# Routed experts of a decoder trunk: one stream over the experts, and the scatter in two rounded products

## The chip, the cores and the metric

The kernel runs on 1 core of one Trainium2 chip. The metric is the device time of one execution in microseconds (us). The kernel before takes 2135.12 us, the median of 3 runs (2126.69 to 2139.0).

## The reference, cut to what matters

A trunk of two layers over 256 tokens of 1024 channels, all in float32. Both layers have the same token mixing (three attention-like mixers between an input and an output projection). The first ends in a dense SwiGLU, the second in a routed one with 8 experts, of which each token uses 2; the change is in that last part.

```python
def swiglu(h, w1, w3, w2):
    return (jax.nn.silu(h @ w1) * (h @ w3)) @ w2

def moe_ffn(h, w_router, w1, w3, w2):
    logits = (h @ w_router).astype(jnp.float32)
    top_v, top_i = lax.top_k(logits, TOP_K)          # TOP_K = 2
    top_w = jax.nn.softmax(top_v, axis=-1)
    gate = jnp.sum(jax.nn.one_hot(top_i, N_EXPERTS) * top_w[..., None], axis=-2)
    y = jnp.zeros_like(h)
    for e in range(N_EXPERTS):                        # 8; w1[e], w3[e]: 1024 x 3584, w2[e]: 3584 x 1024
        y = y + gate[..., e:e + 1] * swiglu(h, w1[e], w3[e], w2[e])
    return y
```

## The kernel before, in words

**Weights.** Every weight passes through one pipe. The SP queue loads it in chunks of 1 MB (128 partitions of 4 rows of 512 columns) into a ring of 6 buffers `raw` (`load`, L539). Each chunk is two halves. For each half ScalarE writes the rounded fp32 copy `w_hi` (L1234, called by `split_to`), and VectorE writes the remainder `w_lo` = `raw` - `w_hi` (L1568). Both have a ring of 4 halves (`HL`), and `split_to` may stand 3 halves (`AHEAD`) ahead of the half that TensorE is to use next. `w_hi` of a half waits until TensorE has used the half that is 4 before it (`half_used`); a `raw` buffer comes free when `w_lo` of both halves is done (`raw_done`). A product is `mm3` (L677 to L679): three rounded-fp32 matmuls per 128 rows of weight, low part of the left side by `w_hi`, high part by `w_lo`, high part by `w_hi`. `use(n)` on ScalarE and VectorE issues the splits up to 3 halves behind the next n chunks and counts them as passed. So splits stand in the same queue as all the other work of these two engines, in the order in which the program is written.

**The experts.** The tokens of one expert (at most 128 in one item) are gathered by a product with a one-hot matrix `sel` (VectorE makes it, L2051): `gather` forms 8 blocks of `x` transposed in the two banks `pT`, VectorE applies the modulation on the way out (`x_f`, L2060, in `gathered`), ScalarE and VectorE split it into `x_hi` and `x_lo` (L2068). Expert width 3584 is cut into 7 blocks of 512. A block has three products of 4 halves, each half 6 matmuls: gate into `pA[0]`, up into `pA[2]`, and down into the two banks `pO`, which stay open over the whole expert. ScalarE takes silu of the gate into `a_sb` (L1520), VectorE multiplies by the up product (`hidden`, L2081), TensorE transposes the result (`turn_a`, L725, 4 transposes in the banks `pT`), ScalarE and VectorE split it into `aT_hi` and `aT_lo` (`hi_a`, and L2089 in `lo_a`). Inside an expert this is staggered: the gate product of block f stands ahead of the transposes of block f - 1, then the up product of f, then the down product of f - 1.

**Between two experts** the order on TensorE is: down product of block 5 of the expert; `gather` for the next expert; `turn_a` of block 6; its down product; then `scatter`, four fp32 matmuls (two instructions each in the trace) of `selT` (the transposed one-hot) and the output `oe` into the banks `pT`, each of which VectorE multiplies by the gate and adds to `yacc` (L2114); then two transposes of the next `sel` into `selT`, and two matmuls by `zeros` that open the banks `pO`; then the gate product of block 0 of the next expert. ScalarE copies the left half of the output out of `pO`, VectorE the right half (L2109). The body of this loop runs `items` times: 8, or 16 if an expert has more than 128 tokens. Here it is 8.

The few lines on TensorE that stand between the experts:

```python
                        with rounds(pe, 1, EFB, {b.raw: 6, b.hl: 12, b.T: 2, G: 1, U: 1, av: 1}):
                            gate_up(pA[0], G, g_free)
                            turn_a()
                            gate_up(pA[2], U, u_free)
                            down()
                        pe.wait_ge(sel_ready, xv.done(v) + 2)
                        gather()
                        turn_a()
                        down(True)
                        evacuated(b.O, O_free, 2)
```

## Time and profile before

| | before |
|---|---|
| median of the runs | 2135.12 us (2126.69 to 2139.0) |
| time of the profiled execution | 2136.17 us |
| its span, from the first to the last instruction | 2134.4 us |
| TensorE matmul busy | 1991.8 us (93%) |
| TensorE weight load busy | 1576.0 us (74%) |
| VectorE busy | 1526.7 us (72%) |
| ScalarE busy | 1237.3 us (58%) |
| mean granted TensorE clock | 0.962 |
| HBM read | 530.83 MB, 249 GB/s over the span |
| the experts | from 1024 us to 2120 us of the span |

The span is read engine by engine: the page's first part gives each engine's busy time, the fourth the chain of work that ended last. An engine with a high share of busy time can still be free at the place where something waits, so the boundaries between experts are read from the timeline. PE stands for TensorE's matmuls, DVE for VectorE, ACT for ScalarE. Starts are us from the start of the span. An execution takes 1.8 us more than its span.

### The profile page before, as it was taken

The numbers are of one execution on the slowest core, as the hardware profiler recorded it, in microseconds if no ns is written. First come the engines' busy times: TensorE is split into PE (matmuls) and PEld (weight loads), VectorE is DVE, ScalarE is ACT, GpSimd is POOL, SyncE is SP. The second block draws the span as 40 slices with busy tenths as digits, with TensorE's granted clock in tenths as the row PEclk, the third lists the DMA queues.
The fourth block names the chain that finished last, engine by engine and source line by source line (L and its number), as shares of the span: only waits on it lengthen the run. The fifth ranks groups of instructions, "written<-read, shape, count | busy, mean of one in ns | idle before, by whom it ended". The sixth has DMA issues, their size and how long they took to land.

```text
span 2134.4 us, 28418 instructions
## 1 busy us (share of the span) xinstructions
PE 1991.8 (93%) x9524; PEld 1576.0 (74%) x9524; DVE 1526.7 (72%) x1827; ACT 1237.3 (58%) x1590; POOL 90.3 (4%) x133
## 2 busy tenths in 40 slices
PE   5999999899979999997899999999999999999996
PEld 2777887777767777886686886877868778687785
DVE  2654565654556644656787897988979888798887
ACT  2544454344324544542576876767767677677773
POOL 0510100000003300000000000000000000000000
PEclk7999999899988999998899999999999999999998
DMA  9656545355734655353597997989979989799892
GB/s 324 218 199 216 179 136 160 115 201 186 257 110 157 234 184 216 119 177 99 189 364 275 352 367 260 363 307 316 365 256 365 328 298 366 258 365 345 289 366 101
DMA packets 275180, 532.74 MB, mean 250 GB/s; under 512 B 10720, under 2 KB 23216, under 8 KB 274992
## 3 DMA queue, kind: packets, MB, share of 16 engines
q1 hardware_dynamic: 275120, 531.91, 71.1%
q8 instruction: 41, 0.67, 0.1%
q14 instruction: 19, 0.16, 0.0%
HBM read 530.83 MB, written 1.05 MB: 249 GB/s over the span
## 4 chain that ended last, share of the span: by engine, by line
PE 84%; DVE 8%; ACT 3%; issue 2%; DVEq 2%; SPq 1%; DMA 0%; ACTq 0%
PE pA L677 17%; PE pA L679 17%; PE pA L678 17%; PE pO L682 6%; PE pO L677 6%; PE pO L679 6%; PE pO L678 6%; PE pT L725 4%; PE pT L682 4%; DVE w_lo L1568 2%; ACT w_hi L1234 1%; PE pA L682 1%; SPq L539 1%; DVE yacc L2114 1%; DVEq L2082 1%
## 5 line engine op out<-in xcount | busy, mean ns | idle before, releaser
L1568 DVE TENSOR_TENSOR w_lo<-raw,w_hi 128x1024 fp32r<-128x1024 f32 x914 | 1093.7, 1225 | 311.5 <-ACT w_hi L1234 290.6
L1234 ACT ACTIVATE w_hi<-raw 128x1024 fp32r<-128x1024 f32 x914 | 957.1, 1058 | 566.8 <-PE pA L679 425.0
L677 PE MATMUL pA<-w_hi,x_lo 128*128 128x512 f32 x896 | 360.3, 402 | 1.7 <-DVE x_lo L2068 0.8
L679 PE MATMUL pA<-w_hi,x_hi 128*128 128x512 f32 x896 | 354.3, 395 | 0.0
L678 PE MATMUL pA<-w_lo,x_hi 128*128 128x512 f32 x896 | 354.0, 395 | 0.0
L677 PE MATMUL pA<-w_hi,h_lo 128*128 128x512 f32 (+2 forms) x736 | 300.2, 408 | 8.3 <-DVE w_lo L1568 8.3
L678 PE MATMUL pA<-w_lo,h_hi 128*128 128x512 f32 (+2 forms) x736 | 290.3, 394 | 0.0
L679 PE MATMUL pA<-w_hi,h_hi 128*128 128x512 f32 (+2 forms) x736 | 289.9, 394 | 0.0
L677 PE MATMUL pO<-w_hi,aT_lo 128*128 128x512 f32 x536 | 218.5, 408 | 19.3 <-DVE yacc L1976 8.8
L678 PE MATMUL pO<-w_lo,aT_hi 128*128 128x512 f32 x536 | 216.4, 404 | 0.0
L679 PE MATMUL pO<-w_hi,aT_hi 128*128 128x512 f32 x536 | 216.3, 404 | 0.0
L677 PEld LDWEIGHTS pA<-w_hi,x_lo 128*128 128x128 f32 x896 | 168.4, 188 | 45.3 <-DVE w_lo L1568 4.4
L679 PEld LDWEIGHTS pA<-w_hi,x_hi 128*128 128x128 f32 x896 | 168.5, 188 | 40.8
L678 PEld LDWEIGHTS pA<-w_lo,x_hi 128*128 128x128 f32 x896 | 168.6, 188 | 37.3
L677 PEld LDWEIGHTS pA<-w_hi,h_lo 128*128 128x128 f32 x736 | 142.6, 194 | 52.9 <-issue 18.8
L679 PEld LDWEIGHTS pA<-w_hi,h_hi 128*128 128x128 f32 x736 | 142.3, 193 | 31.8
L678 PEld LDWEIGHTS pA<-w_lo,h_hi 128*128 128x128 f32 x736 | 142.8, 194 | 27.9
L677 PEld LDWEIGHTS pO<-w_hi,aT_lo 128*128 128x128 f32 x536 | 103.8, 194 | 48.0 <-DVE w_lo L1568 10.8
L679 PEld LDWEIGHTS pO<-w_hi,aT_hi 128*128 128x128 f32 x536 | 103.6, 193 | 25.4
L678 PEld LDWEIGHTS pO<-w_lo,aT_hi 128*128 128x128 f32 x536 | 103.9, 194 | 24.5
L1234 ACT ACTIVATE aT_hi<-pT 128x256 fp32r<-128x256 f32 (+1 forms) x123 | 43.8, 401 | 77.3 <-PE pT L725 77.3
L682 PE MATMUL pO<-raw,csilu 128*32 128x512 f32 x384 | 52.9, 665 | 7.4 <-DMA raw<-in_ada_w 7.4
(228 smaller groups left out, 1713.7 us busy)
## 6 DMA issues: line engine op xcount, KB each, us to landing
raw<-in_moe_w SPq DMA_DIRECT2D x336, 1024.0 KB, 6.8
raw<-in_w_in SPq DMA_DIRECT2D x56, 1024.0 KB, 5.9
raw<-in_ada_w SPq DMA_DIRECT2D x48, 1024.0 KB, 9.3
raw<-in_ffn_w SPq DMA_DIRECT2D x33, 1024.0 KB, 6.2
raw<-in_w_out SPq DMA_DIRECT2D x8, 1024.0 KB, 5.1
raw<-in_cmp_k_w SPq DMA_DIRECT2D x4, 1024.0 KB, 5.3
raw<-in_cmp_v_w SPq DMA_DIRECT2D x4, 1024.0 KB, 10.3
raw<-in_w_read_nsa SPq DMA_DIRECT2D x4, 1024.0 KB, 8.4
```

What stands on the lines that cost most here:

```text
L539: sp.dma_start(slot[:, 0:kb * src.shape[2]].rearrange("p (k n) -> p k n", k=kb), src).then_inc(landed[b.raw.slot(g)], 16)
L677: nc.tensor.matmul(dst, xl, wh, start=first, stop=False, skip_group_check=True)
L678: nc.tensor.matmul(dst, xh, wl, start=False, stop=False, skip_group_check=True)
L679: return nc.tensor.matmul(dst, xh, wh, start=False, stop=last, skip_group_check=True)
L682: return nc.tensor.matmul(dst, lhsT, rhs, start=first, stop=last, skip_group_check=True)
L725: ins = nc.tensor.transpose(pt[0:m, i * width:i * width + n], src, ident[0:n, 0:n])
L1234: return nc.scalar.activation(dst, src, ACT.Copy)
L1568: V.tensor_tensor(w_lo[m][:, 0:n], raw[s][:, i * n:(i + 1) * n], w_hi[m][:, 0:n].bitcast(F32), ALU.subtract).then_inc(raw_done, 1)
L2082: dve.drain().then_inc(u_free, 1)
L2114: V.scalar_tensor_tensor(dst, pt[:, :], gate16[:, t, bass.ds(e, 1)], dst, ALU.mult, ALU.add).then_inc(free, 1)
```

## The change

On TensorE the work of the experts is put in another order; the other engines and the loads follow it.

- The gather for an expert is done a whole expert earlier, and into `pA[1]` and `pA[3]` (which the experts don't use otherwise) in place of the banks `pT`. Ahead of the first expert two gathers are made, the second behind the up product of block 0.
- The gate and up products of block 0 of the next expert stand around the last transposes of the present one, as in an ordinary block: gate of the next, `turn_a` of block 6, up of the next, down of block 6.
- `x_hi` and `x_lo` of the next expert are made while the down product of block 5 runs (`hi_x` on ScalarE, `lo_x` on VectorE).
- The output is split, `oe_hi` by ScalarE and `oe_lo` by VectorE, and `selT` is rounded fp32 as well. The scatter is two rounded-fp32 matmuls (`oe_lo`, then `oe_hi`) into one bank per quarter of the output.
- The gather for the expert after the next stands between the last down product and the scatter; on VectorE `gathered()` stands between `outs` (which makes `oe_lo`) and `scattered` (the sums in `yacc`).
- The transposed one-hot has a matrix `sel_s` of its own. The banks `pO` are opened behind it.
- The loop over the experts is one stream per pass over all 8, with 1 or 2 passes in place of 8 or 16 items. The last expert stands behind the loop. Waits inside it are computed from three loop registers (pass, expert, block) where it were two.

The core of the diff, TensorE:

```diff
-                    pe.wait_ge(sel_ready, 2)
-                    gather()
-                    with rounds(pe, 0, items, {b.raw: 42, b.hl: 84, b.T: 22, b.O: 2, G: EFB, U: EFB, av: EFB, xv: 1}):
-                        v = xv.take()
+                                    ins = mm(pA[1 + 2 * q][:, j * P:(j + 1) * P], y[:, t, k * P:(k + 1) * P], sel[:, t, :], t == 0, t == 1)
+                            ins.then_inc(gather_full, 1)
...
+                    def block():
                         gate_up(pA[0], G, g_free)
+                        turn_a()
                         gate_up(pA[2], U, u_free)
-                        with rounds(pe, 1, EFB, {b.raw: 6, b.hl: 12, b.T: 2, G: 1, U: 1, av: 1}):
-                            gate_up(pA[0], G, g_free)
-                            turn_a()
-                            gate_up(pA[2], U, u_free)
-                            down()
-                        pe.wait_ge(sel_ready, xv.done(v) + 2)
-                        gather()
-                        turn_a()
-                        down(True)
+                        down()
+
+                    def blocks():
+                        open_outs()
+                        with rounds(pe, 1, EFB - 1, {b.raw: 6, b.hl: 12, b.T: 2, G: 1, U: 1, av: 1}):
+                            block()
+                        block()
+
+                    def scatter():
                         evacuated(b.O, O_free, 2)
                         for t in range(TT):
                             for half in range(2):
                                 dst = take_T()
-                                mm(dst[:, :], selT[:, t * P:(t + 1) * P], oe[:, half * W:(half + 1) * W]).then_inc(T_full, 1)
+                                at = slice(half * W, (half + 1) * W)
+                                mm(dst[:, :], selT[:, t * P:(t + 1) * P], oe_lo[:, at], True, False)
+                                mm(dst[:, :], selT[:, t * P:(t + 1) * P], oe_hi[:, at], False, True).then_inc(T_full, 1)
+
+                    with rounds(pe, 0, passes, {b.raw: 42 * NE, b.hl: 84 * NE, b.T: 20 * NE, b.O: 2 * NE, G: EFB * NE, U: EFB * NE,
+                                                av: EFB * NE, xv: NE, gv: NE + 1, sv: NE}):
+                        gather()
+                        first_block()
+                        gate_up(pA[2], U, u_free)
+                        gather()
+                        turn_sel()
+                        with rounds(pe, 0, NE - 1, {b.raw: 42, b.hl: 84, b.T: 20, b.O: 2, G: EFB, U: EFB, av: EFB, xv: 1, gv: 1, sv: 1}):
+                            blocks()
+                            first_block()
+                            turn_a()
+                            gate_up(pA[2], U, u_free)
+                            down(True)
+                            gather()
+                            scatter()
+                            turn_sel()
+                        blocks()
+                        turn_a()
+                        down(True)
+                        scatter()
```

VectorE (`block` is `use(2)`, `lo_a`, `use(2)`, `hidden`):

```diff
+                    def blocks(more):
+                        with rounds(dve, 1, EFB - 1, {b.raw: 6, b.hl: 12, b.hl_in: 12, b.T: 2, av: 1, aq: 2}):
+                            block()
                             use(2)
...
+                        block()
+                        if more:
+                            lo_x()
+                        return use(2)
+
+                    def outs(v):
+                        for half in range(2):
+                            at = slice(half * W, (half + 1) * W)
+                            po, free = O_in(v)
+                            dve.wait_ge(oe_hi_ready, ov.done(ov.take()))
+                            V.tensor_tensor(oe_lo[:, at], po[:, :], oe_hi[:, at].bitcast(F32), ALU.subtract).then_inc(free, 1)
...
+                        one_hot(sel, p * NE, sel_ready)
+                        one_hot(sel_s, p * NE, sel_s_ready)
+                        gathered()
+                        one_hot(sel, p * NE + 1, sel_ready)
+                        lo_x()
+                        use(2)
+                        use(2)
+                        hidden()
+                        gathered()
+                        skip(b.T, 2)
+                        with rounds(dve, 0, NE - 1, {b.raw: 42, b.hl: 84, b.hl_in: 84, b.T: 20, b.O: 2, av: EFB, aq: 2 * EFB, xv: 1, gv: 1, ov: 2}) as e:
+                            at = p * NE + e
+                            one_hot(sel, at + 2, sel_ready)
+                            dve.wait_ge(T_full, b.T.done(b.T.n - 1))
+                            one_hot(sel_s, at + 1, sel_s_ready)
+                            blocks(True)
+                            block()
+                            outs(use(2))
+                            gathered()
+                            scattered(at)
+                            skip(b.T, 2)
```

What this does to the order, at three places. First TensorE between two experts, behind the down product of block 5, in the kernel before (`pT<-sel,y` is the gather, `pT<-tab,a_sb` are the transposes of block 6):

```order
L663 REGISTER_ALU [waits sel_ready]
L682 MATMUL pT<-sel,y 128x128 [waits T_free1]
L682 MATMUL pT<-sel,y 128x128 x7
L663 REGISTER_ALU
L682 MATMUL pT<-sel,y 128x128 [waits T_free0]
L682 MATMUL pT<-sel,y 128x128 x7
L1149 REGISTER_ALU
L725 MATMUL pT<-tab,a_sb 128x128 [waits T_free1,a_ready]
L725 MATMUL pT<-tab,a_sb 128x128
L663 REGISTER_ALU
L725 MATMUL pT<-tab,a_sb 128x128 [waits T_free0]
L725 MATMUL pT<-tab,a_sb 128x128
```

The same transposes in the changed kernel stand between two products of the next expert (`pA<-w_lo,x_hi` ahead of them is its gate, `u_free` behind them opens its up product):

```order
L690 MATMUL pA<-w_lo_60,x_hi 128x512
L691 MATMUL pA<-w_hi_56,x_hi 128x512
L737 MATMUL pT<-tab,a_sb 128x128 [waits T_free1,a_ready]
L737 MATMUL pT<-tab,a_sb 128x128
L675 ISA
L737 MATMUL pT<-tab,a_sb 128x128 [waits T_free0]
L737 MATMUL pT<-tab,a_sb 128x128
L703 ISA [waits u_free]
```

The gather no longer shares `pT` with them, so the transposes wait for nothing of it. Second, TensorE behind the last down product, in the changed kernel (before, `pT<-oe,selT` followed the down product at once):

```order
L1139 REGISTER_ALU [waits sel_ready]
L694 MATMUL pA<-sel,y 128x128 [waits gather_free]
L694 MATMUL pA<-sel,y 128x128 x15
L685 REGISTER_ALU
L694 MATMUL pT<-oe_lo,selT 128x512 [waits T_free1,O_free1,O_free0]
L694 MATMUL pT<-oe_hi,selT 128x512
L675 ISA
L694 MATMUL pT<-oe_lo,selT 128x512 [waits T_free0]
L694 MATMUL pT<-oe_hi,selT 128x512
L694 MATMUL pT<-oe_lo,selT 128x512 [waits T_free1]
L694 MATMUL pT<-oe_hi,selT 128x512
```

The gather has come between the last down product and the scatter. Third, VectorE at the same time, in the changed kernel:

```order
L2180 REGISTER_ALU [waits half_used]
L2181 TENSOR_TENSOR oe_lo<-pO,oe_hi 128x512 [waits oe_hi_ready]
L2180 REGISTER_ALU [waits half_used]
L2181 TENSOR_TENSOR oe_lo<-pO,oe_hi 128x512 [waits oe_hi_ready]
L2131 ISA
L2134 TENSOR_SCALAR x_f<-pA,mod 128x128 [waits gather_full]
L2134 TENSOR_SCALAR x_f<-pA,mod 128x128 x3
L2134 TENSOR_SCALAR x_f<-pA,mod 128x128 [waits gather_full]
L2134 TENSOR_SCALAR x_f<-pA,mod 128x128 x3
L1684 ISA
L2188 ISA [waits T_full]
L2188 SCALAR_TENSOR_TENSOR yacc<-pT,gate_142,yacc 128x512
```

The eight `x_f` of the gather stand between the output's split and the first sum of the scatter; before they stood ahead of the last `aT_lo`.

## Rows read from the trace of the kernel before

**Rows 1.** The page, busy time by engine and the chain that ended last.

```profile
PE 1991.8 (93%) x9524; PEld 1576.0 (74%) x9524; DVE 1526.7 (72%) x1827; ACT 1237.3 (58%) x1590; POOL 90.3 (4%) x133
...
PE 84%; DVE 8%; ACT 3%; issue 2%; DVEq 2%; SPq 1%; DMA 0%; ACTq 0%
```

**Rows 2.** Windows: stretch, us, busy per engine (x), PEclk, DMA share, GB/s.

```profile
1100.00:1148.00 48.00, 48.00 (x214) 38.80 (x213) 43.17 (x43) 38.23 (x43) 0.00 (x0) 1.00 1.01 365
1148.60:1155.30 6.70, 4.45 (x37) 3.93 (x36) 4.76 (x11) 1.31 (x4) 0.00 (x0) 0.97 0.83 307
1155.30:1162.40 7.10, 7.06 (x24) 5.46 (x24) 5.11 (x6) 4.62 (x5) 0.00 (x0) 0.79 0.44 140
1162.40:1169.60 7.20, 4.92 (x14) 1.79 (x13) 4.67 (x6) 2.33 (x4) 0.00 (x0) 1.00 0.50 155
```

**Rows 3.** Timeline of PE between experts 0 and 1: start, us, operation.

```profile
1148.65 3.73 PE L682 MATMUL pT<-sel,y 128*128 128x128 f32 x32
1152.23 0.39 PE L725 MATMUL pT<-tab,a_sb 128*128 128x128 f32 x2
1153.89 0.44 PE L725 MATMUL pT<-tab,a_sb 128*128 128x128 f32 x2 [1.28 <-DVEq L2063]
1155.34 0.79 PE L677 MATMUL pO<-w_hi,aT_lo 128*128 128x512 f32 x1 [1.01 <-DVE aT_lo L2089]
1155.93 0.63 PE L678 MATMUL pO<-w_lo,aT_hi 128*128 128x512 f32 x1
1156.36 0.63 PE L679 MATMUL pO<-w_hi,aT_hi 128*128 128x512 f32 x1
...
1162.13 0.39 PE L679 MATMUL pO<-w_hi,aT_hi 128*128 128x512 f32 x1
1164.18 4.04 PE L682 MATMUL pT<-oe,selT 128*128 128x512 f32 x8 [1.66 <-issue]
...
1169.57 0.51 PE L677 MATMUL pA<-w_hi,x_lo 128*128 128x512 f32 x1
```

**Rows 4.** Timeline of PE in an ordinary block: gate, down, gate of the next.

```profile
1114.18 0.39 PE L677 MATMUL pA<-w_hi,x_lo 128*128 128x512 f32 x1
...
1125.82 0.39 PE L677 MATMUL pO<-w_hi,aT_lo 128*128 128x512 f32 x1
...
1131.42 0.39 PE L677 MATMUL pA<-w_hi,x_lo 128*128 128x512 f32 x1
```

**Rows 5.** Timeline of DVE in the same block.

```profile
1126.87 0.68 DVE L2081 TENSOR_TENSOR a_sb<-a_sb,pA 128x512 f32<-128x512 f32 x1
1127.81 4.73 DVE L1568 TENSOR_TENSOR w_lo<-raw,w_hi 128x1024 fp32r<-128x1024 f32 x4 [0.26 <-issue]
```

**Rows 6.** Timeline of DVE between experts 0 and 1.

```profile
1152.43 1.36 DVE L2060 TENSOR_SCALAR x_f<-pT,mod 128x128 f32<-128x128 f32 x4 [0.42 <-PE pT L682]
...
1155.30 1.29 DVE L2068 TENSOR_TENSOR x_lo<-x_f,x_hi 128x512 fp32r<-128x512 f32 x2
...
1163.40 0.68 DVE L2109 COPY oe<-pO 128x512 f32<-128x512 f32 x1
1165.43 1.50 DVE L2114 SCALAR_TENSOR_TENSOR yacc<-pT,gate,yacc 128x512 f32<-128x512 f32 x2 [1.35 <-PE pT L682]
1167.52 1.49 DVE L2114 SCALAR_TENSOR_TENSOR yacc<-pT,gate,yacc 128x512 f32<-128x512 f32 x2 [0.59 <-PE pT L682]
```

**Rows 7.** Timeline of PE at the last expert's end: gather, then the down product.

```profile
2100.75 3.73 PE L682 MATMUL pT<-sel,y 128*128 128x128 f32 x32
...
2107.44 0.79 PE L677 MATMUL pO<-w_hi,aT_lo 128*128 128x512 f32 x1 [1.01 <-DVE aT_lo L2089]
```

**Rows 8.** Timeline of DVE and PE ahead of expert 0: one-hots, `x_lo`, then the first product.

```profile
1024.12 0.48 DVE L2051 TENSOR_SCALAR sel<-tab,slot 128x128 f32<-128x128 f32 x2 [1.04 <-issue]
...
1031.98 1.29 DVE L2068 TENSOR_TENSOR x_lo<-x_f,x_hi 128x512 fp32r<-128x512 f32 x2
...
1033.50 0.50 PE L677 MATMUL pA<-w_hi,x_lo 128*128 128x512 f32 x1 [0.78 <-DVE x_lo L2068]
```

**Rows 9.** Windows of PE over the last down products of experts 0, 5, 6, 7: us, busy (x), PEclk.

```profile
1155.30:1162.40 7.10, 7.06 (x24) 0.79 0.44 140
...
1836.00:1842.90 6.90, 6.45 (x21) 0.75 0.35 115
1972.70:1978.40 5.70, 5.68 (x24) 1.00 0.27 74
2107.40:2114.50 7.10, 7.06 (x24) 0.78 0.00 0
```

**Rows 10.** Groups of DVE from 1170 to 1280: busy, mean ns | idle before.

```profile
L1568 DVE TENSOR_TENSOR w_lo<-raw,w_hi 128x1024 fp32r<-128x1024 f32 x76 | 90.0, 1222 | 12.8 <-ACT w_hi L1234 11.4 <-issue 1.3
```

**Rows 11.** The line of the waits' register work on DVE's queue: ns min/median/max.

```profile
L1565 DVEq FUSED_REGOPS  x528: 85/85/92, 1048.1 to 2099.3; - x176
```

More of the change, by code:

```diff
@@ new lines, in first_block, with turn_a, down @@
+                    def first_block():
+                        pe.wait_ge(x_ready, xv.done(xv.take(), 2))
+                        gate_up(pA[0], G, g_free)
+                    def turn_a():
+                        v = av.take()
+                        pe.wait_ge(a_ready, av.done(v))
+                        for q in range(2):
+                            turned([a_sb[:, 0, (2 * q + j) * P:(2 * q + j + 1) * P] for j in range(2)], P)
+                    def down(last=False):
+                        evacuated(b.T, T_free, 2)
+                        for half in range(2):
+                            for i in range(2):
+                                wh, wl = half_in(i)
+                                for j in range(CK // 2):
+                                    k = i * (CK // 2) + j
+                                    ins = mm3(outs[half][:, :], aT_hi[:, k, 0:P], aT_lo[:, k, 0:P],
+                                              wh[:, j * W:(j + 1) * W], wl[:, j * W:(j + 1) * W], False, last and k == CK - 1)
+                                ins.then_inc(half_used, 1)
@@ new lines, in outs @@
+                    def outs():
+                        act.wait_ge(half_used, b.hl.done(b.hl.n - 1))
+                        for half in range(2):
+                            v = b.O.take()
+                            copy(oe_hi[:, half * W:(half + 1) * W], pO[b.O.slot(v)][:, :]).then_inc(oe_hi_ready, 1)
+                        skip(b.T, 4)
+                    with rounds(act, 0, passes, {b.raw: 42 * NE, b.hl: 84 * NE, b.hl_in: 84 * NE, b.T: 20 * NE, b.O: 2 * NE, G: EFB * NE,
+                                                 gv: NE + 1}) as p:
+                        hi_x()
@@ new lines, in gathered, with lo_x, hidden @@
+                        dve.drain().then_inc(gather_free, 1)
+                    def lo_x():
+                        v = xv.take()
+                        for q in range(2):
+                            dve.wait_ge(x_hi_ready, xv.done(v, 2) - 1 + q)
+                            V.tensor_tensor(x_lo[:, 4 * q:4 * q + 4, :], x_f[:, 4 * q:4 * q + 4, :],
+                                            x_hi[:, 4 * q:4 * q + 4, :].bitcast(F32), ALU.subtract).then_inc(x_ready, 1)
+                    def hidden():
+                        v = av.take()
+                        dve.wait_ge(g_free, av.done(v))
+                        dve.wait_ge(half_used, b.hl.done(b.hl.n - 1))
+                        V.tensor_tensor(a_sb[:, 0, :], a_sb[:, 0, :], pA[2][:, :], ALU.mult).then_inc(a_ready, 1)
+                        dve.drain().then_inc(u_free, 1)
@@ L2092, in _, with block @@
+                            v = aq.take()
+                            dve.wait_ge(aT_hi_ready, aq.done(v))
+                            V.tensor_tensor(aT_lo[:, 2 * q:2 * q + 2, 0:P], pt[:, 0:SEQ].rearrange("p (k n) -> p k n", k=2),
+                                            aT_hi[:, 2 * q:2 * q + 2, 0:P].bitcast(F32), ALU.subtract).then_inc(free, 1)
+                    def block():
+                        use(2)
+                        lo_a()
+                        use(2)
                         hidden()
-                        dve.wait_ge(T_full, b.T.done(b.T.n - 1))
@@ L2101, in _ @@
[L2101 to L2109 removed]
+                        block()
+                        if more:
+                            lo_x()
```

239 lines of the change are left out of this document (111 added, 128 removed).

## The prediction, made before the changed kernel was run

> **What bounds the kernel now.** I read the page first. TensorE is busy 93% of the span and makes 84% of the chain that ended last [rows 1], so time can only be won where TensorE stands still or runs slowly, or by giving it less to do. The windows come next, since the experts are over half of the span. Within an expert TensorE is busy without a gap at full clock [rows 2], as its first row says; in the 21 us between two experts it is not, as the other three say. The timeline gives the grain: in an ordinary block the down product, 24 matmuls, takes 1131.42 - 1125.82 = 5.60 us, or 0.233 us each, and the block from gate to gate 17.24 us [rows 4]. That is 72 x 0.233 + 0.44, so the four transposes of `turn_a` cost 0.44 us where they stand between two products. Between experts 0 and 1 the last ordinary product ends at 1148.65 and the next expert's first starts at 1169.57 [rows 3]: 20.92 us, of which 5.60 us is a down product at full clock. **15.3 us are lost**, in this order:
>
> - 3.6 us gather (1148.65 to 1152.23);
> - 3.1 us until the down product starts (1155.34). Transposes of the second pair wait 1.28 us for VectorE's drain: the gather and the transposes share `pT`, and VectorE stands in `x_f` [rows 6]. The down product then waits 1.01 us for `aT_lo`.
> - 1.4 us by the clock: the down product's 23 steps from 1155.34 to 1162.13 take 6.79 us in place of 5.37. The granted clock of that stretch is 0.79 [rows 2]: some matmuls run at 1.2 GHz (0.43 us apart, 1155.93 to 1156.36) and the rest at 2.4. What TensorE did before the clock fell was little: two pairs of transposes with 1.28 and 1.01 us of idleness [rows 3].
> - 7.2 us from the last down product to the next first one: `oe`, scatter, next `selT`.
>
> The same sequence stands at all seven boundaries and, without the last item, at the end of expert 7. The clock fell at the last down products of experts 0 to 5 and 7 (0.75 to 0.79; the first, the sixth and the last stand in [rows 9]); at the one of expert 6 it was 1.00 and the product took 5.7 us.
>
> **The change, part by part.**
>
> *Transposes.* They now lie between the next expert's gate and up products, with `pT` free, as in an ordinary block: 0.44 us [rows 4] for 3.1. The low clock that followed them there goes too.
>
> *`x_lo` moves* under the down product of block 5, on VectorE. In an ordinary block VectorE starts `a_sb` 1.05 us after the down product's start and four `w_lo` at 1.99 [rows 4, 5]. The first of the four is for the down product's own fourth half: done at 3.2, needed at 4.2. Two `x_lo` are 1.4 us (the row counts the pair) [rows 6], so it comes 0.35 us late. I price **0.35 us**; bounds are 0, if ScalarE and VectorE overlap better, and 1.4. Afterwards VectorE catches up, for it is idle 12.8 us in 110 us [rows 10], 2.0 us a block.
>
> *From the last down product to the next first product.* The gather is 3.6 us of TensorE, but VectorE sets the end here. Its four `w_lo` end at 1127.81 + 4.73 = 1132.54 in an ordinary block, 1.1 us after the down product [rows 4, 5]; I take 1.5, for what is left of the delay by `x_lo`. Then `oe_lo`, twice, priced as the copy of the same shape, 0.68 us [rows 6]: 2.9 us. Then eight `x_f`, 2 x 1.4 us [rows 6], with a register step: 5.8. Then four sums, 2 x 1.5 us [rows 6]: 8.8. From the end of the last sum (1169.01) to the first product it was 0.56 us before [rows 3, 6], with the same transposes and zeros between: **9.4 us**. TensorE meanwhile gathers, does two scatter products, and waits for VectorE's sums to free `pT`. Bounds: 9.0 (VectorE free at 1.1), 10.5 (oe split waits for ScalarE a second time).
>
> So a boundary costs 0.44 + 0.35 + 9.4 = 10.2 us beside its products, against 15.3 at six boundaries and 13.9 at the one without low clock. The gain is 6 x 5.1 + 3.7 = **34.3 us**, before any new fall of the clock.
>
> *Scatter in two rounded products.* A quarter of the output took two recorded fp32 matmuls, all eight 4.04 us with the waits between them [rows 3]. Now it takes two rounded ones at 0.233 us. The sums on VectorE, 3.0 us, are the longer side, so I take nothing for it. The Trainium skill ("FP8 and Floating Point Precision", TensorE Precision Notes) says that true fp32 takes four passes through the array; by that each of 32 quarters would save two passes, 15 us in all, if TensorE set the pace here. The trace shows pairs of sums, not matmuls, in front of the second half of the scatter, so the sum above stands without it.
>
> *Last expert.* Gather and wait were 2107.44 - 2100.75 = 6.7 us, and 1.4 for the clock as at the boundary [rows 7, 9]. Now there is no gather; transposes 0.44 and the way through `aT_hi` and `aT_lo`, 1155.34 - 1153.89 = 1.45 us [rows 3], make 1.9. The scatter ends 0.4 us later, because VectorE must subtract two halves (2 x 0.68) where it copied one. Gain 6.7 + 1.4 - 1.9 - 0.4 = **5.8 us**.
>
> *Start.* `x_lo` ended the wait for the first product. Ahead of it now stand two more one-hots of 128x128 (the two before took 0.48 us): 0.6 us with their issue [rows 8]. Behind the first up product come a second gather, 3.6 us, and transposes and zeros, 0.6, that were hidden under the wait before. Cost **4.8 us**.
>
> *The clock.* This is the unknown. In the new boundary TensorE has some 5 us (from its second scatter product to the next first product) with about 1.6 us of work: twice 0.47 for scatter, then transposes and zeros. Before, a similar stretch (1152.23 to 1155.34, 0.8 us busy) was followed by a fall seven times in eight [rows 9]. From below I bound it at 0 (as with expert 6), from above at two falls of 1.4 each. Part of a fall should pass while TensorE idles anyway, so I take **0.9 us at each of seven**, 6.3 us.
>
> *Costed at nothing:* ScalarE's second output copy and `x_hi` (ScalarE waits for TensorE in every half; it is busy 38 of 48 us [rows 2]); the loads. The transfers run at 365 GB/s with full share inside an expert [rows 2] and refill during the boundaries. An expert is 44 MB, or 121 us at that rate, and is to take some 131, so the six buffers still refill.
>
> **Sum:** 34.3 + 5.8 - 4.8 - 6.3 = 29.0 us. Span 2134.4 - 29.0 = 2105.4; with the 1.8 us around it **2107 us**. The profiled execution (2136.17) lies 1.05 us above the median of the runs shown, so against that the gain is 28 us, 1.3%. Changes below 0.5% (10.7 us) could not be told from none here.
>
> **Rivals.**
>
> *The clock stays up.* Then 6.3 us more are won: **2101 us**. For it: behind expert 6 nothing fell after the same waits [rows 9]; the clock also stayed 1.00 over 1162.4 to 1169.6, which held idle stretches of its own [rows 2]. Against it: the new stretch has less work. The Trainium skill ("TensorE: Matmul & The Clock Gate", Why this matters for your kernels) warns only of single idle gaps longer than any that I forecast here. By that rule this rival holds; but the trace has falls after gaps of 1.28 and 1.01 us, so the trace speaks against the rule. 17%.
>
> *VectorE does not catch up.* Each boundary puts `x_lo`, eight `x_f`, one-hots and sums in the queue of `w_lo`, and the ring is only 3 halves deep. If TensorE waits for `w_lo` some 3 us more at each of the eight starts, 24 us are given back: **2131 us**, no difference. Against it: 2.0 us idle per block [rows 10]. 7%.
>
> *Waits from three registers.* Every split waits for a value computed from loop registers; now there are three. Such a step is 85 ns on VectorE's queue [rows 11] and hidden behind the instruction in progress. VectorE has about 15 in a block, and 2.0 us to spare [rows 10]. It decides from 0.13 us more per wait; with 0.26 us (the "issue" gap of [rows 5]) a block grows by 15 x 0.26 - 2.0 = 1.9 us, and 56 blocks by 106: **2213 us**, slower. Against it: the order of the changed program shows one register step per wait as before. 4%.
>
> **How the numbers follow.** The forecast has 72%. Its own range is 2097 to 2122: at best VectorE is free early (7 x 0.4) and the clock falls little; at worst `x_lo` costs 1.4 at each boundary (7 x 1.05), `oe_lo` waits (7 x 1.1). The first rival lies inside. I give 2096 to 2122. Faster needs under 2124.4: nearly all of the forecast and all of the first rival, 0.89. The second rival is the middle, 0.07; the third is slower, 0.04.
>
> **What would show it.** In the profile after: block period still 17.24 us; transposes of block 6 without a wait; a boundary whose last down product is followed by gather and, behind VectorE's sums, by the next product after 9 to 10 us; expert period about 130 us for 136. Wrong would be: TensorE waiting for `w_lo` inside ordinary blocks, ScalarE waiting for DMA, or a boundary over 13 us.

## The result, and the profile after

| | before | changed |
|---|---|---|
| median of the runs, us | 2134.57 (2126.69 to 2139.0) | 2103.39 (2101.57 to 2107.42) |
| profiled execution / its span, us | 2136.17 / 2134.4 | 2101.57 / 2099.8 |
| start of the first gather, us | 1024.86 | 1022.43 |
| first gather to VectorE's first product with `gw`, us | 1095.6 | 1063.5 |

The ratio is 0.9861, 95% interval 0.9828 to 0.9893: 31 us less, where 28 were forecast against the median. The spans differ by 34.6 us. Of these 2.4 stand ahead of the experts, where the program is the same: over all kernels of this study the first gather starts between 1015 and 1025 us. What the change did is read in the last row of the table: **32.2 us less**, where the sum of the forecast was 29.0. `gw` is the factor by which VectorE multiplies `yacc` as soon as the last expert's sums are done, so this stretch holds all eight experts. The later experiments are compared by it ("the expert stretch"), since their times carry the same 10 us of noise from ahead of it. It comes from one profile of each kernel. Two profiles of the changed kernel gave 1063.5 and 1063.4 us, but inside them the clock fell at different places, at 1.0 to 1.5 us each time, so a difference of 1 or 2 us is read together with the clock.

The page of the changed kernel, which answers to [rows 1]:

```profile
PE 1967.5 (94%) x9524; PEld 1568.3 (75%) x9524; DVE 1527.9 (73%) x1849; ACT 1222.1 (58%) x1582; POOL 90.3 (4%) x133
...
PE 84%; DVE 8%; ACT 3%; issue 2%; DVEq 1%; DMA 1%; SPq 0%; ACTq 0%
```

The shares hardly moved: TensorE's busy time fell by 24 us and its idle time by 10. Neither tells where. The windows do (stretch, us, busy per engine, PEclk, DMA share, GB/s); they answer to [rows 2]:

```profile
1100.00:1140.00 40.00, 40.00 (x179) 32.33 (x179) 35.82 (x35) 31.24 (x36) 0.00 (x0) 1.00 1.03 369
1168.50:1178.20 9.70, 7.31 (x45) 5.18 (x43) 8.55 (x19) 1.64 (x4) 0.00 (x0) 0.94 0.60 219
1178.20:1182.00 3.80, 3.80 (x14) 3.04 (x13) 1.33 (x2) 2.08 (x2) 0.00 (x0) 0.72 0.00 0
1310.20:1314.00 3.80, 3.80 (x17) 3.09 (x17) 2.25 (x2) 2.82 (x3) 0.00 (x0) 1.00 0.07 4
```

Inside an expert nothing changed. The boundary is 9.7 us long, and VectorE is busy for 8.55 of them: it is now the fuller engine there. Behind the first boundary the clock is at 0.72, behind the second at 1.00. Over that first boundary TensorE's timeline reads, to be held against [rows 3]:

```profile
1156.87 0.60 PE L737 MATMUL pT<-tab,a_sb 128*128 128x128 f32 x4
...
1168.51 3.73 PE L694 MATMUL pA<-sel,y 128*128 128x128 f32 x32
1172.00 0.48 PE L694 MATMUL pT<-oe_lo,selT 128*128 128x512 f32 x1
...
1174.84 0.50 PE L694 MATMUL pT<-oe_lo,selT 128*128 128x512 f32 x1 [1.68 <-DVE yacc L2188]
...
1176.62 0.30 PE L737 MATMUL pT<-tab,sel_s 128*128 128x128 f32 x1 [0.39 <-DVE yacc L2188]
1177.19 0.48 PE L737 MATMUL pT<-tab,sel_s 128*128 128x128 f32 x1 [0.27 <-DVE yacc L2188]
1177.72 1.03 PE L694 MATMUL pO<-zeros 128*128 128x512 bf16 x2
```

The transposes of block 6 wait for nothing. From the end of the last down product (1168.51) to the next first product (1178.22) it is 9.71 us, and every wait names VectorE's sums. VectorE's own timeline over the same stretch, against [rows 6], shows what stands ahead of them:

```profile
1164.91 4.72 DVE L1640 TENSOR_TENSOR w_lo<-raw,w_hi 128x1024 fp32r<-128x1024 f32 x4 [0.27 <-issue]
1169.55 1.28 DVE L2181 TENSOR_TENSOR oe_lo<-pO,oe_hi 128x512 fp32r<-128x512 f32 x2
1170.74 1.36 DVE L2134 TENSOR_SCALAR x_f<-pA,mod 128x128 f32<-128x128 f32 x4
1172.28 1.37 DVE L2134 TENSOR_SCALAR x_f<-pA,mod 128x128 f32<-128x128 f32 x4 [0.18 <-PE pA L694]
1174.03 1.41 DVE L2188 SCALAR_TENSOR_TENSOR yacc<-pT,gate,yacc 128x512 f32<-128x512 f32 x2 [0.39 <-issue]
1175.72 1.41 DVE L2188 SCALAR_TENSOR_TENSOR yacc<-pT,gate,yacc 128x512 f32<-128x512 f32 x2 [0.28 <-PE pT L694]
```

The start, against [rows 8], and the last expert, against [rows 7], on TensorE:

```profile
1022.43 5.88 PE L694 MATMUL pA<-sel,y 128*128 128x128 f32 x32 [3.30 <-DVE sel L2124]
1031.88 0.49 PE L689 MATMUL pA<-w_hi,x_lo 128*128 128x512 f32 x1 [3.56 <-DVE x_lo L2143]
1043.17 3.73 PE L694 MATMUL pA<-sel,y 128*128 128x128 f32 x32
...
2071.24 0.60 PE L737 MATMUL pT<-tab,a_sb 128*128 128x128 f32 x4
2073.16 0.49 PE L689 MATMUL pO<-w_hi,aT_lo 128*128 128x512 f32 x1 [1.31 <-DVE aT_lo L2158]
2081.07 0.47 PE L694 MATMUL pT<-oe_lo,selT 128*128 128x512 f32 x1 [2.06 <-DVE oe_lo L2181]
```

### The profile page after: what moved, and what is told of

The parts are those of the page before. It is cut to its first block, busy times and chain, and to the rows that moved or that the text cites. A ratio compares the mean times of both kernels' runs of the same rounds, so it can differ in the third digit from the quotient of the medians.

```text
span 2099.8 us, 28335 instructions
## 1 busy us (share of the span) xinstructions
PE 1967.5 (94%) x9524; PEld 1568.3 (75%) x9524; DVE 1527.9 (73%) x1849; ACT 1222.1 (58%) x1582; POOL 90.3 (4%) x133
## 4 chain that ended last, share of the span: by engine, by line
PE 84%; DVE 8%; ACT 3%; issue 2%; DVEq 1%; DMA 1%; SPq 0%; ACTq 0%
PE pA L689 18%; PE pA L691 18%; PE pA L690 18%; PE pO L694 7%; PE pO L689 6%; PE pO L691 5%; PE pO L690 5%; PE pT L737 4%; DVE w_lo L1640 2%; PE pA L694 2%; PE pT L694 1%; ACT w_hi L1281 1%; DMA raw<-in_ada_w 1%; DVE yacc L2188 1%; DVEq L2151 0%
## 5 line engine op out<-in xcount | busy, mean ns | idle before, releaser
L689 PE MATMUL pA<-w_hi,h_lo 128*128 128x512 f32 (+2 forms) x736 | 299.1, 406 | 10.5 <-DVE w_lo L1640 10.4
L689 PE MATMUL pO<-w_hi,aT_lo 128*128 128x512 f32 x536 | 213.1, 398 | 13.7 <-DVE yacc L2048 8.8
L690 PE MATMUL pO<-w_lo,aT_hi 128*128 128x512 f32 x536 | 211.8, 395 | 0.0
L691 PE MATMUL pO<-w_hi,aT_hi 128*128 128x512 f32 x536 | 211.8, 395 | 0.0
```

The source lines that it names most:

```text
L689: nc.tensor.matmul(dst, xl, wh, start=first, stop=False, skip_group_check=True)
L690: nc.tensor.matmul(dst, xh, wl, start=False, stop=False, skip_group_check=True)
L691: return nc.tensor.matmul(dst, xh, wh, start=False, stop=last, skip_group_check=True)
```

## The experiments

"Boundary" is the time from the end of an expert's last down product to the next expert's first product not yet done.

**The scatter alone, undone.**

```diff
-    mm(dst, selT, oe_lo[:, at], True, False)
-    mm(dst, selT, oe_hi[:, at], False, True).then_inc(T_full, 1)
+    mm(dst, selT, oe[:, at]).then_inc(T_full, 1)          # fp32
```

> The changed kernel, only with the scatter as it was: one true-fp32 product per quarter of the output, selT and oe in fp32, VectorE copying one half of oe where it subtracts two. My theory: VectorE sets the end of a boundary (8 x_f, then 4 sums), so the boundary (last down product's end to the next first product) stays at 9.7 us within 0.4; TensorE's quarters grow from 0.47 us by some 0.4 each but lie beside VectorE, which has 0.7 less to do. Time 2100 to 2106 us, as the changed kernel (2103.4). Rival: TensorE's longer quarters set the end; then each of 32 quarters adds some 0.4 us and the time is about 2116 us, with a boundary of 11 us or more.

Measured: 2100.76 us, 0.9864 of before (0.9835 to 0.9894); the expert stretch is 1061.6 us, **1.9 less** than in the changed kernel. The boundary is 10.16 us, 0.45 more, but the clock falls at none of the seven:

```profile
1165.90:1176.00 10.10, 8.49 (x45) 5.19 (x43) 8.20 (x18) 1.15 (x3) 0.00 (x0) 1.00 0.52 198
1176.10:1180.00 3.90, 3.90 (x18) 3.16 (x18) 2.38 (x2) 2.96 (x3) 0.00 (x0) 1.00 0.02 6
```

The longer fp32 quarters lie mostly in time that TensorE would have waited, 8.49 us busy for 7.31, and what they add is given back by the clock. The times, 2100.76 against 2103.39 us and 2099.95 in the repeat below, cannot be told apart. So the rounded scatter won nothing in this change.

**The scatter alone, done** to the kernel before (`oe_hi` by ScalarE, `oe_lo` by VectorE, two products per quarter; the reverse of the diff above).

> The kernel before, only with the scatter in two rounded products (oe_hi by ScalarE, oe_lo by VectorE). My theory: nothing to be seen, 2132 to 2138 us; the stretch from the last down product to the next first product stays at 7.2 us within 0.5, since 0.7 us more on VectorE stands against shorter quarters between sums. Rival: TensorE's passes set this stretch; two of four passes saved in 32 quarters give some 13 us, 2121 us and a stretch of 5.6 us.

Measured: 2136.92 us, 1.0029 of before (1.0008 to 1.005); expert stretch 1100.2 us, **4.6 more**. The rival is out. My own figure missed by half a microsecond per expert: from the last down product to the next first product it takes 7.7 us where it took 7.2 [rows 3]. VectorE has a second half to subtract ahead of the sums: the first quarter starts 2.65 us behind the start of the last product ahead of it, where it was 2.05 [rows 3]. The clock also falls a second time. The last steps of the down product are back at full speed, and the quarters are not, where the whole stretch had 1.00 before [rows 2]:

```profile
1149.00:1152.80 3.80, 3.80 (x18) 2.88 (x16) 2.52 (x3) 2.94 (x3) 0.00 (x0) 1.00 0.77 258
1155.60:1160.40 4.80, 4.18 (x11) 2.08 (x10) 2.98 (x4) 0.32 (x2) 0.00 (x0) 0.64 0.30 115
```

Of the 4.6 us, 1.35 are neither: in this profile the clock fell at expert 6's last down product too (7.21 us), where it had stayed up before (5.86 us).

**VectorE's order.** The same instructions, two calls exchanged on one engine:

```diff
-                            gathered()
                             scattered(at)
+                            gathered()
```

> The changed kernel with two calls exchanged on VectorE alone: the four sums of the scatter ahead of the eight x_f. TensorE's order is untouched. My theory: VectorE's 2.8 us of x_f ahead of the sums set the end of the boundary; without them the sums start when the first scatter quarter is done (4 us after the last down product) and the next first product starts after 8.1 us in place of 9.7. Seven boundaries give 11 us: 2092 us (2088 to 2096). Rival A: TensorE sets the end (gather, four quarters, transposes); then the boundary stays 9.7 us and the time 2103. Rival B: the x_f now stand in front of w_lo of the next expert, and TensorE waits for w_lo inside its first gate product; the boundary gets shorter but the first block longer by as much, 2100 to 2103.

Measured: 2087.73 us, 0.9805 of before (0.9771 to 0.984); expert stretch 1053.6 us, **9.9 less** than the changed kernel for 11 forecast; the time lies just below my range. The boundary is 8.51 us. VectorE:

```profile
1163.89 1.28 DVE L2181 TENSOR_TENSOR oe_lo<-pO,oe_hi 128x512 fp32r<-128x512 f32 x2
1167.22 1.41 DVE L2188 SCALAR_TENSOR_TENSOR yacc<-pT,gate,yacc 128x512 f32<-128x512 f32 x2 [2.04 <-PE pT L694]
1168.91 1.41 DVE L2188 SCALAR_TENSOR_TENSOR yacc<-pT,gate,yacc 128x512 f32<-128x512 f32 x2 [0.28 <-PE pT L694]
1170.24 2.64 DVE L2134 TENSOR_SCALAR x_f<-pA,mod 128x128 f32<-128x128 f32 x8
```

It now waits 2.04 us for TensorE's gather and first quarter, and the eight `x_f`, which nobody needs for another expert, stand behind the sums. That VectorE's order set the end of the boundary is shown: nothing else was touched. The terms: 7 x 1.2 us by the boundary (8.5 for the 8.1 forecast), three falls of the clock fewer at 1.0 us, and back 0.2 us in each second block, where `w_lo` now comes late. The last is Rival B, at a sixth of the size it would need.

**Without the next expert's products around the last transposes.**

```diff
 blocks()
-first_block()
 turn_a()
-gate_up(pA[2], U, u_free)
 down(True)
 gather()
 scatter()
 turn_sel()
+first_block()
+gate_up(pA[2], U, u_free)
```

(and likewise on the other engines and in the order of the loads).

> The changed kernel without the next expert's first products around the last transposes: transposes of block 6, down product, gather, scatter, then the next expert's gate and up products; the gather still has banks of its own and stands behind the down product. My theory: the transposes again wait for ScalarE and VectorE, 1.9 us to the down product as at the last expert, in place of 0.44, so 1.5 us at each of seven boundaries, less the 0.35 us of the x_lo stall: about 8 us by these, 2111 us; a low clock in the down product behind the wait would add up to 1.4 us at each, 2121 us. Range 2108 to 2122. Rival: the separate banks alone gave the whole gain, 2103 us or less, with transposes that wait for nothing.

Measured: 2117.64 us, 0.9939 of before (0.9917 to 0.9961); expert stretch 1078.5 us, **15.1 more** than the changed kernel. The transposes stand in front of a wait again. Of expert 1:

```profile
1283.76 0.60 PE L737 MATMUL pT<-tab,a_sb 128*128 128x128 f32 x4
1286.43 0.70 PE L689 MATMUL pO<-w_hi,aT_lo 128*128 128x512 f32 x1 [2.08 <-DVE aT_lo L2161]
```

The low clock behind the wait is not back, except at this expert. The windows of the last down products of experts 0, 1 and 2, of which the other five are like the first:

```profile
1150.90:1156.80 5.90, 5.89 (x26) 4.82 (x27) 3.73 (x4) 3.19 (x3) 0.00 (x0) 1.00 0.99 362
1286.40:1293.80 7.40, 7.37 (x26) 5.90 (x27) 3.69 (x4) 3.18 (x3) 0.00 (x0) 0.77 0.82 299
1421.10:1427.00 5.90, 5.90 (x26) 4.79 (x27) 3.73 (x4) 3.18 (x3) 0.00 (x0) 1.00 1.00 366
```

So 15.1 of the 32.2 us hang on the stream of products; the other 17.1 are what all the rest of the change wins together. The largest part of them that rows show is the clock: a last down product takes 5.86 us at seven experts, where 7.2 to 7.4 us stood at seven experts before [rows 9]: six falls fewer, about 9 us in all. The transposes and the wait are the same in kind; what is gone from ahead of them is the gather. That the gather's place decides this is not shown by a run that moves it alone, but the ninth experiment, which keeps the gather there, keeps six of the eight falls that it could have.

Between boundaries without a fall the period is 133.1 us, 2.2 more than in the changed kernel, where my theory had 1.2: from the start of the transposes to the down product it is 2.67 us, where the transposes cost 0.44 in a stream. The first period is 136.7 us; its 3.6 us more are two stretches of low clock, behind the first boundary and in expert 1's down product.

**The idle stretch filled** with products of zeros, whose result nobody reads.

```diff
+    fill(5)   # ahead of the third quarter; 1 ahead of the fourth, 2 ahead of turn_sel
```

> The changed kernel with 8 matmuls of zeros (128x512 bf16, into the pO banks that the next expert opens anyway) put into TensorE's waits of the boundary: 5 ahead of the third scatter quarter, 1 ahead of the fourth, 2 ahead of selT's transposes. Theory: the clock falls behind a boundary because TensorE does little between its second scatter quarter and the next first product; with the waits filled it stays up. It fell at 4 of 7 boundaries, at about 1.0 us each (expert periods 131.9 against 130.9), so the time from the first gather to the end of the last expert, 1063.5 us in the changed kernel, becomes about 1059.5, with all periods at 130.9; the time 2099 (2097 to 2103). Rival: the falls do not depend on this work; periods go on alternating and the stretch stays 1063 to 1064. A second rival: the filler itself delays the scatter quarters by some 0.2 us each, and the periods are then all 131.5.

Measured: 2098.07 us, 0.9839 of before (0.981 to 0.9867); expert stretch 1059.5 us, **4.0 less**. The boundary did not grow (9.68 us), the clock stands at 1.00 behind all seven and every period is 130.9 us:

```profile
1172.10:1181.80 9.70, 8.68 (x54) 5.80 (x52) 8.63 (x19) 1.64 (x4) 0.00 (x0) 1.00 0.59 214
1181.80:1186.00 4.20, 4.20 (x19) 3.41 (x19) 2.50 (x3) 3.18 (x3) 0.00 (x0) 1.00 0.09 13
```

That the whole stretch hits the forecast is partly luck: expert 0's first products ran at low clock here (1.5 us more), though the first of them came 0.3 us sooner, and from the seventh boundary to the end it took 1.9 us less, of which only some 1.1 are the fourth fall. The six periods between the first and the last boundary hold the effect by itself: 785.3 us for 788.6, 3.3 us for the three falls in them.

**`x_lo` behind two `w_lo`.**

```diff
-    lo_x()
-    return use(2)
+    use(1)
+    lo_x()
+    return use(1)
```

> The changed kernel with VectorE's two x_lo put behind the first two w_lo of the down product of block 5 (they stood ahead of them). Theory: the 0.35 us stall in that down product goes, as its fourth half's w_lo is in time; x_lo is then ready some 0.3 us before the next expert's first product needs it. The stretch from the first gather to the end of the last expert gets 7 x 0.35 = 2.5 us shorter, 1061 us; the time 2101, not to be told from the changed kernel's 2103.4 by time alone, so the trace decides. Rival: the stall moves to the first product, which then waits for x_lo; stretch 1063 to 1066.

Measured: 2108.33 us, 0.9911 of before (0.9883 to 0.9939); expert stretch 1071.1 us, **7.6 more**. A miss: the rival's wait came, and it was larger.

```profile
1144.88 2.36 DVE L1640 TENSOR_TENSOR w_lo<-raw,w_hi 128x1024 fp32r<-128x1024 f32 x2 [0.75 <-ACT w_hi L1281]
1147.15 1.29 DVE L2143 TENSOR_TENSOR x_lo<-x_f,x_hi 128x512 fp32r<-128x512 f32 x2
...
1148.74 0.49 PE L689 MATMUL pA<-w_hi,x_lo 128*128 128x512 f32 x1 [0.58 <-DVE x_lo L2143]
```

I had let VectorE start its two `w_lo` at once, but they wait 0.75 us for ScalarE, a gap in which `x_lo` had stood. The new wait of 0.58 us in place of a stall of 0.35 explains 1.6 us. The rest is mostly low clock: it falls behind five boundaries, and longer, with periods up to 133.7 us. Whether the new wait, some 20 us ahead of the boundary, brought that about stays open.

**The scatter out of the boundary.** TensorE's order for one expert; the others follow.

```diff
 block(); first_block(); turn_a(); gate_up(pA[2], U, u_free)
 down(True)
-gather()
-scatter()
 turn_sel()
+gather()
+open_outs()
+block()       # block 1 of the next expert
+scatter(0)    # two quarters
+block()
+scatter(1)    # the other two
```

> The changed kernel with VectorE taken off the end of the boundary: behind the last down product stand only selT's transposes and the gather, then the next expert's products; the scatter and its sums go into the gaps behind blocks 1 and 2 of the next expert, two quarters in each. Theory: a boundary is then TensorE's own work, 0.6 + 3.6 + zeros 0.5 = 4.7 us in place of 9.7, with 2.1 us of scatter in the blocks and no clock fall (0.6 a boundary on average). 3.5 us at each of seven boundaries: 24 us less, 2079 us (2074 to 2086); the stretch from the first gather to the end of the last expert 1039 us in place of 1063.5. Rival: VectorE has oe_lo, x_f and the new sums in front of w_lo, and TensorE waits for w_lo in the first blocks, 2 to 3 us at each boundary: 2095 to 2100.

Measured: 2071.94 us, 0.9734 of before (0.9714 to 0.9755); expert stretch 1032.5 us, **31.0 less** than the changed kernel where 24 were forecast, and the time is below my range. A boundary takes 4.03 us and has no wait:

```profile
1166.31 0.38 PE L737 MATMUL pT<-tab,sel_s 128*128 128x128 f32 x2
1166.53 3.73 PE L694 MATMUL pA<-sel,y 128*128 128x128 f32 x32
1170.10 0.59 PE L694 MATMUL pO<-zeros 128*128 128x512 bf16 x2
...
1187.77 0.40 PE L694 MATMUL pT<-oe_lo,selT 128*128 128x512 f32 x1
```

The period is 127.2 us for 131.4 on average, 4.2 less and not 3.5: I had put 0.6 + 3.6 + 0.5 us for these three operations, but without waits between them they overlap, and a pair of quarters takes 0.93 us. The rival, VectorE late with `w_lo`, did not come: no `w_lo` wait beyond the one of block 5.

**The same, with the scatter in true fp32** (the first diff on top of the last).

> The same as the run before it, with the scatter in true fp32 (one product per quarter, oe and selT in fp32). Theory: where TensorE alone sets the pace, the number of passes counts, which it did not at the boundary of the changed kernel: 32 quarters at 0.86 us in place of 0.47 make 12 us, so 2091 us (2087 to 2094). VectorE has 0.7 us less to do at each boundary, which should not show. Rival: it is as in the changed kernel, no more than 2 us either way.

Measured: 2081.39 us, 0.9773 of before (0.9755 to 0.9791); expert stretch 1043.2 us, **10.7 more** than with rounded products, for 12 forecast. The time is below my range, which I had built on 2079 us for the run before; that one took 2071.94. Two quarters:

```profile
1182.76 1.88 PE L693 MATMUL pT<-oe,selT 128*128 128x512 f32 x4
```

The next product starts 1.31 us behind their start, for 0.93 with rounded ones, and is itself 0.80 us long for 0.39: 0.8 us per pair, 0.39 per quarter. A quarter is 0.86 us for 0.47, a ratio of 1.8. The Trainium skill ("FP8 and Floating Point Precision", TensorE Precision Notes) gives true fp32 four passes. If each of the two rounded products counts as one pass, an estimate by it is a ratio of 2; the trace comes near. The same edit was worth nothing where VectorE set the end of the stretch.

**The gather's banks alone,** in the kernel before.

```diff
-    pt = take_T()
-    ins = mm(pt[:, j * P:(j + 1) * P], y[...], sel[:, t, :], t == 0, t == 1)
+    ins = mm(pA[1 + 2 * q][:, j * P:(j + 1) * P], y[...], sel[:, t, :], t == 0, t == 1)
```

> The kernel before, only with its gather in banks of its own (pA[1] and pA[3], free in the experts) in place of the two pT banks; the order of work stays on every engine. My prediction blamed the 1.28 us wait of the second transposes on the shared pT. Theory A, by VectorE's order: aT_lo stands behind the second four x_f on VectorE (done at 1153.8 in the kernel before, 1.5 us after the gather), so the down product starts only some 0.4 us earlier, 6.3 us behind the start of the gather in place of 6.7; 8 x 0.4 = 3 us, 2128 us, not to be told from before by time. Theory B, by the shared banks: the wait goes, the down product starts 5.4 us behind the gather, and with it the low clock: 8 x 1.3 + 7 x 1.4 = 20 us, 2111 us.

Measured: 2128.24 us, 0.9982 of before (0.9963 to 1.0); expert stretch 1091.9 us, **3.8 less**. The down product starts 6.35 us behind the gather's start:

```profile
1144.44 3.73 PE L684 MATMUL pA<-sel,y 128*128 128x128 f32 x32
1148.02 0.60 PE L727 MATMUL pT<-tab,a_sb 128*128 128x128 f32 x4
1150.80 0.78 PE L679 MATMUL pO<-w_hi,aT_lo 128*128 128x512 f32 x1 [2.18 <-DVE aT_lo L2092]
```

All four transposes run at once, and TensorE waits 2.18 us in one piece where it waited 1.28 and 1.01 [rows 3]. Theory A: what was late was `aT_lo`, behind `x_f` on VectorE. The shared banks only decided in front of which instruction TensorE stood. Of the 3.8 us, 1.5 are one fall of the clock fewer: the last down product takes 5.86 us at experts 3 and 6 here, at expert 6 alone before, and 7.2 to 7.4 us at the others. That leaves 2.3 us for the 3 of Theory A.

**The better version,** and the changed kernel once more.

```diff
 for q in range(2):
+    if between and q:
+        split_to(b.hl.n + AHEAD + 1)      # one w_lo between the two x_lo
```

> The kernel with the scatter behind blocks 1 and 2 (e7_spread), and one w_lo between the two x_lo. Theory: the fourth half of block 5's down product is then delayed by 0.64 us where two x_lo delayed it by 1.29, and its stall of 0.35 us goes; x_lo is ready 1.5 us before it is needed, so there is no wait as when both stood behind two w_lo. 7 x 0.35 = 2.5 us: the stretch from the first product to the first product with gw 1020.6 us in place of 1023.05, an expert period 126.85 us in place of 127.20; the time 2069.5 (2065 to 2074), not to be told from 2071.9 by time alone. Rival: either wait is left, period 127.2.

Measured: 2063.63 us, 0.9681 of before (0.966 to 0.9703); expert stretch 1031.0 us, 1.5 less than without it, for 2.5; the period is 126.9 us, as forecast. The time is 1.4 us below my range and 8.3 below the seventh experiment. The two profiles show only 1.5 us of that, in the expert stretch; no row shows the rest, and this edit is not credited with it. The wait of block 5 is gone from the trace, and TensorE has nothing left but its own work (1 ms of the experts; 344 GB/s):

```profile
1040.00:2040.00 1000.00, 999.89 (x4542) 810.49 (x4540) 914.34 (x980) 769.02 (x873) 0.00 (x0) 1.00 0.96 344
```

> The changed kernel itself, unchanged, for its spread from run to run. Up to the experts nothing was changed, yet the profiled runs reach the first gather between 1015 and 1025 us. I expect a time of 2098 to 2108 us; the stretch from the first product of the experts to the first product with gw 1054 us within 2; the clock falls behind the boundaries again at some of the seven, not at the same ones if they depend on what the chip does, at the same ones if they follow from the kernel alone.

Measured: 2099.95 us, 0.9845 of before (0.9819 to 0.9871); expert stretch 1063.4 us, as at first (1063.5). But the clock fell behind the other boundaries: 0.81 behind the second, 1.00 behind the first, the reverse of the first profile. The equal sum hides unequal parts: expert 0's first products ran at a low clock here, 1.5 us more, and the last expert ended 1.8 us earlier.

```profile
1178.20:1182.00 3.80, 3.80 (x18) 3.06 (x18) 2.32 (x2) 2.87 (x3) 0.00 (x0) 1.00 0.04 6
1310.20:1314.00 3.80, 3.80 (x15) 3.06 (x14) 2.05 (x2) 1.65 (x2) 0.00 (x0) 0.81 0.27 60
```

## Why the prediction was right, term by term

2107 us were forecast and 2103.4 measured, inside the range and by the likeliest case. Its terms against the expert stretch:

| term | forecast, us | measured, us |
|---|---|---|
| seven boundaries, before the clock | 34.3 | 32.2 |
| last expert | 5.8 | 5.1 |
| start | -4.8 | -4.9 |
| new low clock | -6.3 | -4.0 |
| one-hots ahead of `w_lo`, before | not in the sum | 3.0 |
| sum | 29.0 | 31.4 |

The stretch shows 32.2; 0.8 us are left without a row. The mechanism was right at the boundary: the places of the gather, the transposes and VectorE's queue. The closeness of the sum is partly luck: the boundaries were priced 2.1 us too high as a gain and the new low clock 2.3 too high as a loss, which cancel, and the one-hots were not seen at all.

*Boundaries.* 0.44 for the transposes held, and so did 0.35 for `x_lo`: one wait of 0.17 us in front of the fourth half of block 5's down product, which takes 5.9 to 6.0 us for 5.60. From the last down product to the next first one it was 9.71 us for 9.4. VectorE was free after 1.1 us where I took 1.5, and its last sum ended after 8.6 where I took 8.8. But from there to the first product it takes 1.09 us for 0.56: the zeros now follow behind a loop's jump instead of directly behind the transposes. That is argued from the order of the program; no run moved them alone. 7 x 10.5 us against 6 x 15.3 + 13.9 make 32.2.

*Last expert.* The wait was 1.9 us, as forecast. The way from the last down product to the end of the sums is 6.9 us for 5.8 before, not 0.4 but 1.1 more: the scatter's products run at a clock of 0.76, which I had not put there. In the repeat of the changed kernel they ran at full clock and it was 6.15 us, the 0.4 of the forecast. Start: 9.45 us to the first product for 8.64, and 4.04 for the second gather with transposes and zeros.

*The clock.* It fell behind four boundaries of seven in this profile, at 1.0 us each by the periods (131.95 against 130.95 us), where I took seven at 0.9. That a fall costs about 1 us and follows from little work in the waits, the filled boundary supports: eight products of zeros and no fall in its one profile, against four and three falls in the two profiles of the changed kernel, where a fall cost 1.0 and 1.2 us. Not every gap with little work is followed by one: the wait of 2.08 us behind the transposes in the fourth experiment was at one expert of eight. The 17% rival, a clock that stays up, was not so in the changed kernel and is so in that one and in four others (the first, seventh, eighth and tenth experiments). The rule of the Trainium skill ("TensorE: Matmul & The Clock Gate", Why this matters for your kernels), which warns of long single gaps, is again not what the trace shows: the longest gap of the boundary is 1.68 us, and the clock falls.

*Not in the sum.* In the kernel before, VectorE made the one-hots in the second block of each expert ahead of four `w_lo`, and TensorE lost 0.38 us there: the product at 1184.85 is followed by one at 1185.36, then 1185.70, for a spacing of 0.233. I had read one ordinary block and took the block behind a boundary for another such. The changed kernel makes the one-hots at the boundary. 8 x 0.38 = 3.0 us. VectorE's timeline there, in the kernel before:

```profile
1183.62 0.48 DVE L2051 TENSOR_SCALAR sel<-tab,slot 128x128 f32<-128x128 f32 x2 [0.35 <-issue]
1184.08 4.63 DVE L1568 TENSOR_TENSOR w_lo<-raw,w_hi 128x1024 fp32r<-128x1024 f32 x4
```

Nothing is idle between the two rows, and TensorE goes on when the first of the four `w_lo` ends: its loss comes from an engine that is simply busy, which is why no wait names it. This is read from the two timelines, alike at all eight experts; no run moved the one-hots alone.

*The scatter.* Priced at nothing, and right: by the pair of experiments it adds 4.6 us to the kernel before (3.2 without the fall at expert 6) and 1.9 to the changed one. A gain from shorter products comes only where TensorE sets the pace: there it was 10.7 us, where the prediction had 15 by the passes.

*The cause I had wrong.* "The gather and the transposes share `pT`" was my reading of the 1.28 us wait. The wait named VectorE's queue, and VectorE stood in `x_f` either way: banks alone won 0.34 us of it. The forecast did not suffer, since the change also moved the gather away. The low clock behind that wait I had put down to "two pairs of transposes" and their idleness; the fourth and ninth experiments point to the gather ahead of them as well.

*The other rivals.* VectorE catches up: no wait for `w_lo` but the one forecast. Waits from three registers cost nothing: an ordinary block still takes 17.24 us.

## What to carry to other kernels

When two engines share a short stretch, add up each one's queue in its order and look at what stands ahead of the result that the other waits for: here a swap of two calls on VectorE won 10 us (3 of them by the clock), and shorter scatter products on TensorE won none until VectorE was out of the way. A stretch between two loops is best emptied into the blocks around it, where the engine that sets the pace has no waits to share; that made 2063.6 us of 2103.4, with 32.5 of the 39.8 us in the expert stretch; no row shows the rest. Read the first block behind a boundary too, not just an ordinary one.

## What the runs showed of the hardware that I had not expected

- The clock falls at every second boundary of the same kernel: behind the first, third, fifth and seventh in one profile, behind the second, fourth and sixth in the other. The program is the same, so it does not decide alone which boundary is hit.
- Four transposes and then 2.1 us of waiting for `aT_lo`: with the gather's 32 small products ahead of them (3.7 us) the clock fell in six of eight down products behind (the ninth experiment), with a down product of 128x512 matmuls ahead in one of eight (the fourth).
- A slower instruction need not cost time: with fp32 products the boundary is 0.45 us longer, the clock stays at 1.00 behind all seven in that profile, and the stretch is 1.9 us shorter.
- 344 GB/s are held for 1 ms with TensorE at 999.89 of 1000 us: the transfers, at a share of 0.96, did not become the bound, though six buffers are all that stands ahead of them.
